# Decode's set-up and first page loads placed in the last heads of prompt attention, sums of probabilities inverted through 32x32 turns, in a hybrid attention and MLP step

## The chip, the cores and the metric

One core of one Trainium2 chip. The metric is the device time of the whole program in microseconds. In these texts PE is TensorE (PEld its weight loads), DVE VectorE, ACT ScalarE, POOL GpSimd, and SP SyncE, whose queue issues the DMAs.

## The reference

One layer of an inference step over a prompt of 16 + 1024 tokens and over 8 sequences with 4 new tokens each, whose past lies in pages:

```python
q, lat, kpe, gb, u = _mixer_inputs(hp, w_in, ...)          # prompt
k, v = _expand_kv(lat, kpe, w_ukv, k_norm_g)
attn = _prompt_attention(q, k, v)                          # 8 heads, causal softmax
xp = _merge_and_ffn(xp, attn, conv, ...)                   # w_o, then a squared-ReLU MLP
# sampled tokens, for each of 8 sequences: 32 pages of 128 past tokens, and 4 new ones
lat_all = concatenate([cache_lat[pages].reshape(past, KV_LORA), lat])
kp_all = concatenate([cache_kpe[pages].reshape(past, QK_ROPE), kp])
k, v = _expand_kv(lat_all, kp_all, w_ukv, k_norm_g)        # keys are RMS-normalised per head
s = where(mask, einsum('qhd,khd->hqk', qs, k) * ATTN_SCALE, -inf)
attn = einsum('hqk,khd->qhd', softmax(s), v)
```

## The kernel before

The program runs five phases in turn, each a block of one instruction stream for every engine, with a barrier of all engines behind each: `inputs`, `prompt_attention`, `sample_attention`, `output_and_mlp`, `store_outputs`. Prompt and sampled tokens share all of them but the two attentions. Within an engine's stream the order is written out by hand, and semaphores couple the engines.

**Prompt attention** goes over heads n = 0 to 7 and, in each, over six steps ("go" 0 to 5). While a head's values are multiplied, the next head's scores are made and the keys and queries of the one after it are turned and split into a rounded and a rest part. In a step PE makes two score blocks of head n+1 (L1325), turns a unit of head n+2 (L1305), and adds two blocks of values of head n (L1361); ACT copies scores out of the accumulators (L1146), exponentiates (L1151) and copies outputs and sums of probabilities (`keep_output`, L1158, L1159); DVE subtracts maxima (L1258) and keeps running ones (L1245, L1247). The sums stand in `g.sums`, 1040 columns on 128 partitions, where all 64 rows of a head hold the same numbers. Heads come in pairs, and in heads 2, 4 and 6 DVE also inverts the sums of the pair before, half a chunk in each of the six steps (`invert_sums`, L1269); POOL then multiplies the outputs (L1103). In head 6 there is no unit to turn, in head 7 no scores are made either. The last pair's inversion stands in the next phase.

**Sample attention** starts with set-up. SP loads the page table and the weight `w_ukv`, then pages, a latent and a rope part each. PE turns 16 pieces of the weight (L1828), ACT copies them (L1554), PE forms the queries in latent space (L1835), DVE and ACT copy and split them (L1645, L1562, L1650) and the weight (`comb_hi` L1557, `comb_lo` L1654), and ACT spreads the rope part (L1564). Then the 32 new tokens' own block: their key norms (L1838, L1560, L1567), scores, mask, maximum, exponential, and first context (L1843 to L1705). DVE's stream also holds the last pair's inversion (L1642) and its multiplication (L1697). All of this stands ahead of the first page. After it come 32 groups of 8 pages: for each page PE turns it (L1896) and expands it to keys and scores (L1906, 12 matmuls), ACT squares (L1614), DVE reduces (L1796). A group's softmax and its context are run one group later. Page buffers are four sets of 8.

## Time and profile before

| | us |
|---|---|
| median of 3 runs (lowest, highest) | 2009.86 (2008.13, 2009.87) |
| profiled execution | 2010.35 |
| its span in the profile | 2008.6 |
| PE busy in the span | 1914.7 |
| DVE, ACT, POOL busy | 962.9, 738.1, 453.9 |

The span runs from the first to the last recorded instruction; the execution's own time is 1.75 us more. The busy times overlap. A duration with "x4" behind it is that of four instructions run one after the other, and a bracket at the end of a row gives the idle time of the engine ahead of it and what ended it.

### The profile page before, as it was taken

The page shows a single profiled execution, that of the slowest core. Times are in us where ns is not written, and L with a number is a line of the kernel's source. Part 1 is how long each engine was busy: PE and PEld are TensorE (multiplying, and loading weights), DVE is VectorE, ACT ScalarE, POOL GpSimd, SP SyncE. Part 2 cuts the span into 40 slices and gives each one's busy share as a digit, 9 for nine tenths or more (in the row PEclk, how much of TensorE's full clock was granted, in tenths as well). Part 3 has the DMA queues.
Part 4 walks back from the last instruction along what each step waited for, and adds up shares of the span by engine and source line. Part 5 has one row for each costly group of instructions (what it writes and reads, how often), then busy time and mean ns, then how long its engine had stood idle before and what let it go on. Part 6 is the DMA issues. An engine that isn't in the chain of part 4 may idle for free. (4 is left out here: it accounts for less than half of the span.)

```text
span 2008.6 us, 36206 instructions
## 1 busy us (share of the span) xinstructions
PE 1914.7 (95%) x12672; PEld 1808.8 (90%) x12672; DVE 962.9 (48%) x1710; ACT 738.1 (37%) x1532; POOL 453.9 (23%) x433
## 2 busy tenths in 40 slices
PE   6999997999779999999998699999999999999998
PEld 5999996777569999999997499999999999999998
DVE  6115034788657777777777733323222322223132
ACT  5111223666446666666666332111111111111011
POOL 3242233232200000000100444222222222122221
PEclk8999998999879999999999599999999999999999
DMA  6122000000122222222222111020211112020202
GB/s 223 43 66 74 11 12 17 1 0 1 39 77 66 74 73 71 71 73 73 73 73 101 42 43 53 18 68 27 58 40 44 52 31 64 24 78 10 73 16 102
DMA packets 180603, 108.47 MB, mean 54 GB/s; under 512 B 52132, under 2 KB 177154, under 8 KB 180276
## 3 DMA queue, kind: packets, MB, share of 16 engines
q1 hardware_dynamic: 180358, 107.21, 18.6%
q8 instruction: 46, 0.75, 0.2%
q10 hardware_dynamic: 174, 0.30, 0.1%
q14 instruction: 25, 0.20, 0.0%
HBM read 97.47 MB, written 10.00 MB: 54 GB/s over the span
## 5 line engine op out<-in xcount | busy, mean ns | idle before, releaser
L1906 PE MATMUL banks<-comb_hi,pageT_hi 128*128 128x272 f32 x1024 | 233.8, 310 | 0.0
L1796 DVE TENSOR_REDUCE k_sums<-k_sq 128x8 f32<-128x512 f32 x256 | 174.3, 681 | 91.3 <-ACT k_sq L1614 91.3
L1906 PE MATMUL banks<-comb_hi,pageT_lo 128*128 128x272 f32 x1024 | 212.3, 289 | 0.0
L1906 PE MATMUL banks<-comb_lo,pageT_hi 128*128 128x272 f32 x1024 | 211.8, 288 | 0.0
L2264 DVE TENSOR_TENSOR xT<-xT,banks 128x1056 f32<-128x1056 f32 x64 | 80.3, 1255 | 272.7 <-PE banks L247 272.7
L1614 ACT ACTIVATE k_sq<-banks 128x512 f32<-128x512 f32 x256 | 152.1, 594 | 141.3 <-PE banks L1906 138.4
L2146 ACT ACTIVATE a_hi<-relu 128x1056 fp32r<-128x1056 f32 x32 | 34.9, 1089 | 388.5 <-DVE relu L2252 388.5
L236 POOL TENSOR_TENSOR w_down_lo<-w_down_raw,w_down_hi 128x512 fp32r<-128x512 f32 x64 | 94.6, 1478 | 339.7 <-ACT w_down_hi L232 339.7
L247 PE MATMUL banks<-hf_hi,w_out_up_hi 128*128 128x352 f32 x768 | 167.1, 326 | 0.0
L247 PE MATMUL banks<-a_lo,w_down_hi 128*128 128x352 f32 x768 | 166.8, 325 | 0.0
L2252 DVE SCALAR_TENSOR_TENSOR relu<-banks,ffn_norm_inv 128x1056 f32<-128x1056 f32 x32 | 40.2, 1258 | 263.8 <-PE banks L247 258.3
L247 PE MATMUL banks<-hf_hi,w_out_up_lo 128*128 128x352 f32 x768 | 166.0, 324 | 0.0
L247 PE MATMUL banks<-a_hi,w_down_lo 128*128 128x352 f32 x768 | 165.8, 324 | 0.0
L247 PE MATMUL banks<-hf_lo,w_out_up_hi 128*128 128x352 f32 x768 | 165.8, 324 | 0.0
L247 PE MATMUL banks<-a_hi,w_down_hi 128*128 128x352 f32 x768 | 165.6, 324 | 0.0
L236 POOL TENSOR_TENSOR w_out_up_lo<-w_out_up_raw,w_out_up_hi 128x1024 fp32r<-128x1024 f32 x40 | 101.5, 2544 | 266.9 <-ACT w_out_up_hi L232 266.9
L1906 PEld LDWEIGHTS banks<-comb_lo,pageT_hi 128*128 128x128 f32 x1024 | 161.3, 189 | 0.0
L1906 PEld LDWEIGHTS banks<-comb_hi,pageT_lo 128*128 128x128 f32 x1024 | 160.7, 189 | 0.0
L1906 PEld LDWEIGHTS banks<-comb_hi,pageT_hi 128*128 128x128 f32 x1024 | 157.7, 190 | 0.0
L247 PEld LDWEIGHTS banks<-hf_hi,w_out_up_hi 128*128 128x128 f32 x768 | 131.4, 190 | 1.1 <-issue 1.1
L247 PEld LDWEIGHTS banks<-hf_hi,w_out_up_lo 128*128 128x128 f32 x768 | 132.3, 188 | 0.0
L247 PEld LDWEIGHTS banks<-a_hi,w_down_hi 128*128 128x128 f32 x768 | 131.4, 188 | 0.0
(382 smaller groups left out, 3813.6 us busy)
## 6 DMA issues: line engine op xcount, KB each, us to landing
page_latents<-in_cache_kv_latent SPq DMA_DIRECT2D x256, 128.0 KB, 2.1
w_out_up_raw<-in_w_up SPq DMA_DIRECT2D x32, 512.0 KB, 4.1
w_down_raw<-in_w_down SPq DMA_DIRECT2D x64, 256.0 KB, 2.7
w_in_raw<-in_w_in SPq DMA_DIRECT2D x17, 512.0 KB, 3.9
x_spill<-xT SPq DMA_DIRECT2D x1, 4296.0 KB, 15.2
xT<-x_spill SPq DMA_DIRECT2D x1, 4296.0 KB, 13.8
page_ropes<-in_cache_k_rope SPq DMA_DIRECT2D x256, 16.0 KB, 1.8
w_out_up_raw<-in_w_o SPq DMA_DIRECT2D x8, 512.0 KB, 4.1
```

Source lines behind the costliest of these rows:

```text
L236: nc.gpsimd.tensor_sub(self.lo[s][:, :, :], self.raw[s][:, :, :], self.hi[s][:, :, :].bitcast(F32)).then_inc(self.lo_done[s], 1)
L247: mm = pe.matmul(out[:, b, 0:self.tb], w[s][:, k, :], x(k)[:, b * self.tb:(b + 1) * self.tb], start=k == 0 and a == 0, stop=k == self.K - ...
L1614: act.activation(sq[j % 2][:, :].rearrange("p (a c) -> p a c", a=2), kn[:, :, 0:WK], ACT.Square)\
L1796: nc.vector.tensor_reduce(ksum[par][:, j, :], sq[j % 2][:, :].rearrange("p (h c) -> p h c", h=H), AX_X, ALU.add)\
L1906: mm = pe.matmul(banks[:, 2 * (j % 2) + half, 0:WC], x[j % AHEAD][:, k, :], w[par][:, k, half, :], start=k == 0 and a == 0, stop=k == KL - ...
L2146: act.activation(a_hi[:, f, :], relu[:, f % 2, :], ACT.Square).then_inc(hi_done, 1)
L2252: nc.vector.scalar_tensor_tensor(blocked(relu[:, s, :]), slot(s)[:, :, 0:OB], 0.0, inv, ALU.max, ALU.mult)\
L2264: nc.vector.tensor_add(x, x, slot(s)[:, :, 0:OB]).then_inc(down.evacuated[s], 1)
```

## The change

The set-up is taken out of `sample_attention`. `prompt_attention` gets an SP stream, which loads `w_ukv` and the page table once head 7's units are turned, and the first two groups of pages once POOL has prepared head 7's values. PE turns the weight in steps 2 to 5 of head 6 (`turn_w`) and forms the latent queries in steps 0 to 3 of head 7; ACT and DVE copy and split beside it, `comb_hi`, `ropes_of_queries`, `strip_fold` and `comb_lo` in head 7. Behind head 7 stand the split of the latent queries and the inversion of the last pair's first chunk (columns 640 to 1039).

`invert_sums` turns a chunk's sums in 32x32 blocks, inverts one column of each block, and turns the inverses back with the one column read 32 times; three DVE instructions a chunk take the place of two reciprocals.

In `sample_attention` the new tokens' block is spread over the page steps of group 0 and the start of group 1 (`new_block`, `new_context`), all in accumulator bank 7. The remaining 640 columns of the last pair are inverted by five reciprocals between the reductions of group 0, and POOL multiplies all 1040 columns in group 1. POOL's constants follow its first copies. The buffers of the moved tensors lie where the token-major queries, keys and values lay.

```diff
+def load_page(g, sp, n, j, q, latents, ropes):
+    lat_cache, rope_cache = g.A["cache_kv_latent"], g.A["cache_k_rope"]
+    page = sp.value_load(g.pages[0:1, ds(n, 1)], min_val=0, max_val=lat_cache.shape[0] - 1)
+    sp.dma_start(latents[:, j, 0:KVL], lat_cache[ds(page, 1), :, :].rearrange("o p n -> p (o n)")).then_inc(g.pages_loaded[q], 16)
+    sp.dma_start(ropes[:, j * ROPE:(j + 1) * ROPE], rope_cache[ds(page, 1), :, :].rearrange("o p n -> p (o n)"))\
+        .then_inc(g.ropes_loaded[q], 16)
...
+    g.sums = low.take("probability_sums", [P, TP + SW - TP % SW], F32)
+    turned_sums = ar.take("turned_sums", [P, (TP - 640) // SW + 1, SW], F32)
+    sum_inv = ar.take("sum_inverses", [P, (TP - 640) // SW + 1], F32)
...
+        @block.sync
+        def _(sp):
+            sp.wait_ge(s["unit_transposed"], H * NU)
+            sp.dma_start(g.wkv[:, :, :], A["w_ukv"].rearrange("(k p) n -> p k n", p=P)).then_inc(s["w_loaded"], 16)
+            sp.dma_start(g.pages[:, :], A["page_table"]).then_inc(s["table_loaded"], 16)
+            sp.wait_ge(s["table_loaded"], 16)
+            sp.wait_ge(s["v_head_ready"], H)
+            for q in range(2):
+                for j in range(PAGE_GROUP):
+                    load_page(g, sp, q * PAGE_GROUP + j, j, q, g.early_pages[q], g.early_ropes[q])
+            sp.wait_ge(s["w_loaded"], 16)
...
+            def keep_w(x):
+                act.wait_ge(s["wT_done"], x + 1)
+                act.copy(g.wukT[0:NOPE, 4 * x:4 * x + 4, :].rearrange("p a c -> p (a c)"), banks[0:NOPE, UNIT_BANK, :])\
+                    .then_inc(s["wT_copied"], 1)
+            def comb_hi(p):
+                act.wait_ge(s["w_loaded"], 16)
+                act.copy(g.comb_hi[p][:, :, :, 0:WK].rearrange("p k a (h c) -> p (k a) h c", c=NOPE),
+                         nope[:, :, 0:NOPE].rearrange("p (a h) c -> p a h c", h=H // 2)).then_inc(s["comb_w_hi"], 1)
+            def ropes_of_queries():
+                act.wait_ge(s["unit_lo_done"], H * NU)
+                for quad in range(4):
+                    act.copy(g.qr4[quad * ROPE:(quad + 1) * ROPE, :, :].rearrange("p b (h s) -> p b h s", h=H),
+                             g.qs[NOPE:QK, :, :].rearrange("p h (b s) -> p b h s", s=SDEC)).then_inc(s["qr_copied"], 1)
...
+                    if is_head(n, H - 2) and go >= 2:
+                        keep_w(go - 2)
+                    if is_head(n, H - 1) and go < 2:
+                        comb_hi(go)
+                    if is_head(n, H - 1) and go == 2:
+                        ropes_of_queries()
...
+                if is_head(n, H - 1):
                     keep_output(n, par, pair, 2)
+                    act.wait_ge(s["qab_copied"], KL)
+                    act.copy(g.qab_hi[:, :, :, :], g.qab[:, :, :, :]).then_inc(s["qab_split"], 1)
...
             def invert_sums(pair, go):
-                c, half = go // 2, go % 2
+                c, back = go // 2, go % 2
                 q0, q1 = CHUNKS[c]
-                mid = (q0 + q1) // 2
-                if half == 0:
+                n = -(-(q1 - q0) // SW)
+                sums = g.sums[:, q0:q0 + n * SW]
+                turn = turned_sums[:, 0:n, :]
+                if not back:
                     v.wait_ge(s["out_copied"], (pair * 2 + 1) * NC + (c + 1))
-                cols = slice(mid, q1) if half else slice(q0, mid)
-                nc.vector.reciprocal(g.sums[:, cols], g.sums[:, cols]).then_inc(s["sums_inverted"], 1)
+                    nc.vector.transpose(turn.rearrange("p a b -> p (a b)"), sums).then_inc(s["sums_turned"], 1)
+                else:
+                    v.wait_ge(s["sums_turned"], pair * NC + (c + 1))
+                    nc.vector.reciprocal(sum_inv[:, 0:n], turn[:, :, 0:1].rearrange("p a o -> p (a o)")).then_inc(s["sums_found"], 1)
+                    v.wait_ge(s["sums_found"], pair * NC + (c + 1))
+                    nc.vector.transpose(sums.rearrange("p (a b) -> p a b", b=SW), sum_inv[:, 0:n].unsqueeze(2).broadcast_to([P, n, SW]))\
+                        .then_inc(s["sums_inverted"], 1)
+            def comb_lo(p):
...
+            def latents_of_queries():
+                v.wait_ge(s["qab_done"], 1)
+                for k in range(KL):
+                    nc.vector.tensor_copy(g.qab[:, :, k, :].rearrange("p b (h s) -> p b h s", h=H),
+                                          banks[:, UNIT_BANK, k * H * NS:(k + 1) * H * NS]
+                                          .rearrange("p (h b s) -> p b h s", b=NSEQ, s=SDEC)).then_inc(s["qab_copied"], 1)
+                v.wait_ge(s["qab_copied"], KL)
+                v.wait_ge(s["qab_split"], 1)
+                nc.vector.tensor_sub(g.qab_lo[:, :, :, :].rearrange("p b k q -> p (b k q)"),
+                                     g.qab[:, :, :, :].rearrange("p b k q -> p (b k q)"),
+                                     g.qab_hi[:, :, :, :].bitcast(F32).rearrange("p b k q -> p (b k q)")).then_inc(s["qab_lo_done"], 1)
             def loop(n, par, pair, norm):
                 if isinstance(n, int) and n == -1:
...
+                    if is_head(n, H - 1) and go == 1:
+                        strip_fold()
+                    if is_head(n, H - 1) and go in (2, 3):
+                        comb_lo(go - 2)
+                if is_head(n, H - 1):
+                    latents_of_queries()
+                    invert_sums(pair, 0)
+                    invert_sums(pair, 1)
...
+            def turn_w(x):
+                if x == 0:
+                    pe.wait_ge(s["w_loaded"], 16)
+                    pe.wait_ge(s["unit_lo_done"], H * NU)
+                else:
+                    pe.wait_ge(s["wT_copied"], x)
+                for i in range(4):
+                    h, k = (4 * x + i) // KL, (4 * x + i) % KL
+                    mm = pe.transpose(banks[0:NOPE, UNIT_BANK, i * P:(i + 1) * P], g.wkv[:, k, h * KW:h * KW + NOPE], ident[:, :])
+                mm.then_inc(s["wT_done"], 1)
+            def latents_of_queries(x):
+                if x == 0:
+                    pe.wait_ge(s["wT_copied"], 4)
+                for h in (2 * x, 2 * x + 1):
+                    for k in range(KL):
+                        at = k * H * NS + h * NS
+                        mm = pe.matmul(banks[:, UNIT_BANK, at:at + NS], g.wukT[0:NOPE, h * KL + k, :], g.qs[0:NOPE, h, :],
+                                       start=True, stop=True)
+                if x == 3:
+                    mm.then_inc(s["qab_done"], 1)
...
+            for q in range(2, SETS):
+                for j in range(G):
+                    load_page(g, sp, q * G + j, j, q, X[q], R[q])
+            with sp.Fori(1, GROUPS // SETS) as i:
                 for q in range(SETS):
+                    sp.wait_ge(s["pages_free"][q], i + 1)
                     for j in range(G):
-                        page = sp.value_load(pages[0:1, ds(i * (SETS * G) + (q * G + j), 1)], min_val=0,
-                                             max_val=n_pool - 1)
-                        if j == 0:
...
+                if is_second(n):
+                    x = g.attnT[:, AW // P - 1, 0:TP]
+                    pool.wait_ge(s["prompt_sums_inverted"], SUM_PIECES)
+                    nc.gpsimd.tensor_mul(x, x, g.sums[:, 0:TP]).then_inc(s["prompt_normed"], 1)
...
+            def new_block(j):
+                s0 = f8(st, NS)
+                s04 = st[0:NS, :, :].rearrange("p b (h s) -> p b h s", h=H)
+                s0T = banks[0:HS, 7, 0:NSEQ * NS].rearrange("p (b t) -> p b t", b=NSEQ)
+                if j == 0:
+                    rope = g.new_page[:, KVL:KVL + ROPE]
+                    nc.vector.tensor_mul(diag[:, :], rope, rope).then_inc(s["k0_parts"], 1)
+                    v.wait_ge(s["k0_parts"], 1)
+                    nc.vector.reduce_sum(rsum[0:NS, 0:1], diag[:, :], AX_X).then_inc(s["k0_parts"], 1)
+                    v.wait_ge(s["sq0_done"], 1)
+                    nc.vector.tensor_reduce(ksum[1][0:NS, 0, :], sq0.rearrange("p (h c) -> p h c", h=H), AX_X, ALU.add)\
+                        .then_inc(s["k0_parts"], 1)
+                    v.wait_ge(s["k0_parts"], 3)
+                    nc.vector.tensor_scalar(rk[0:NS, 0:H], ksum[1][0:NS, 0, :], rsum[0:NS, 0:1], 1.0 / QK, ALU.add, ALU.mult)\
+                        .then_inc(s["k0_parts"], 1)
+                    v.wait_ge(s["k0_parts"], 4)
+                    nc.vector.tensor_scalar(rk[0:NS, 0:H], rk[0:NS, 0:H], EPS, None, ALU.add).then_inc(s["k0_mean"], 1)
+                if j == 2:
+                    v.wait_ge(s["k0_root"], 1)
+                    nc.vector.reciprocal(rk[0:NS, 0:H], rk[0:NS, 0:H]).then_inc(s["k0_inv"], 1)
+                    v.wait_ge(s["s0_done"], 1)
+                    nc.vector.tensor_copy(s0, banks[0:NS, 7, 0:NSEQ * HS]).then_inc(s["s0_steps"], 1)
+                    v.wait_ge(s["s0_steps"], 1)
...
+            def new_context_kept():
+                v.wait_ge(s["l0_done"], 1)
+                v.wait_ge(s["ctx0_copied"], 8)
+            def invert_sums(x):
+                cols = slice(x * P, (x + 1) * P)
+                nc.vector.reciprocal(g.sums[:, cols], g.sums[:, cols]).then_inc(s["prompt_sums_inverted"], 1)
             def soft_mean(n, par):
...
+                    if is_first(n):
+                        new_block(j)
+                        if j in (0, 1, 3, 5, 7):
+                            invert_sums((j + 1) // 2)
+                    if is_second(n) and j == 7:
+                        new_context_kept()
...
+            def new_block(j):
+                if j == 0:
+                    for k in range(KL):
+                        mm = pe.matmul(banks[0:NS, 7, :], g.new_latT[:, k, :], nope[:, k * H:(k + 1) * H, 0:NOPE],
+                                       start=k == 0, stop=k == KL - 1)
+                    mm.then_inc(s["kn0_done"], 1)
+                if j == 1:
+                    pe.wait_ge(s["sq0_done"], 1)
+                    for k in range(KL):
+                        pe.matmul(banks[0:NS, 7, 0:NSEQ * HS], g.new_latT[:, k, :], qab[:, :, k, :], start=k == 0, stop=k == KL - 1)
+                    pe.matmul(banks[0:NS, 7, NSEQ * HS:2 * NSEQ * HS], g.kpe_s[NOPE:QK, :],
+                              g.qs[NOPE:QK, :, :].rearrange("p h (b s) -> p b h s", s=SDEC), start=True, stop=True)\
+                        .then_inc(s["s0_done"], 1)
+                if j == 4:
+                    pe.wait_ge(s["s0_steps"], 4)
+                    for b in range(NSEQ):
+                        mm = pe.transpose(banks[0:HS, 7, b * NS:(b + 1) * NS], st[0:NS, b, :], ident[0:NS, 0:NS])
+                    mm.then_inc(s["s0_transposed"], 1)
+                if j == 6:
+                    pe.wait_ge(s["s0_shifted"], 1)
+                    pe.matmul(banks[:, 7, 2 * NSEQ * NS - NSEQ:2 * NSEQ * NS], fold[0:HS, :, :].rearrange("p a q -> p (a q)"),
+                              mrun[0:HS, :], start=True, stop=True).then_inc(s["m0_spread"], 1)
+                if j == 7:
+                    pe.wait_ge(s["m0_done"], 1)
+                    pe.wait_ge(s["p0_done"], 1)
+                    for b in range(NSEQ):
+                        mm = pe.transpose(banks[0:NS, 7, b * HS:(b + 1) * HS], sc[1][0:HS, b, :], ident[0:HS, 0:HS])
+                    mm.then_inc(s["p0_transposed"], 1)
+            def new_context():
+                pe.wait_ge(s["p0_copied"], 1)
+                pe.wait_ge(s["m0_done"], 1)
+                for a in range(2):
+                    mm = pe.matmul(banks[:, 7, a * KVL:(a + 1) * KVL], pr[0:NS, 4 * a:4 * a + 4, :].rearrange("p b q -> p (b q)"),
+                                   g.new_page[:, 0:KVL], start=True, stop=True)
+                mm.then_inc(s["ctx0_done"], 1)
             def spread_max(n):
...
+                    if is_second(n) and j == 0:
+                        new_context()
                     if soft is not None:
                         if j == 5:
+                            if is_second(n):
+                                pe.wait_ge(s["ctx0_copied"], 8)
                             transpose_max(soft[0])
                         if j == 6:
```

## Rows read from the trace of the kernel before

**Rows 1.** The page: the span, and busy time of each engine with its share.

```profile
span 2008.6 us, 36206 instructions
...
PE 1914.7 (95%) x12672; PEld 1808.8 (90%) x12672; DVE 962.9 (48%) x1710; ACT 738.1 (37%) x1532; POOL 453.9 (23%) x433
```

**Rows 2.** Busy time by stretch: PE, PEld, DVE, ACT, POOL; TensorE's clock; DMA.

```profile
490.00:530.00 40.00, 36.48 (x185) 26.47 (x184) 32.42 (x75) 24.72 (x46) 8.73 (x12) 0.96 0.00 1
...
545.00:556.31 11.31, 9.36 (x44) 8.52 (x42) 1.45 (x1) 3.75 (x3) 0.00 (x0) 0.50 0.34 90
556.31:575.10 18.79, 8.91 (x33) 3.78 (x32) 11.25 (x24) 7.71 (x15) 2.18 (x7) 0.59 0.31 80
...
575.10:591.30 16.20, 15.54 (x109) 15.17 (x110) 7.32 (x15) 7.41 (x23) 0.00 (x0) 0.84 0.33 85
564.00:575.10 11.10, 3.83 (x22) 2.54 (x22) 7.66 (x20) 3.79 (x9) 2.18 (x7) 0.50 0.31 81
...
607.00:623.00 16.00, 16.00 (x138) 15.11 (x137) 12.55 (x32) 10.93 (x31) 1.44 (x4) 1.00 0.28 74
```

**Rows 3.** Timeline from the last prompt copy to the first page: start, duration, engine, line, [idle].

```profile
537.36 0.37 ACT L1159 COPY attnT<-banks 64x256 f32<-64x256 f32 x1
538.54 0.25 SPq L1469 DMA_DIRECT2D page_table<-in_page_table  x1
...
539.80 6.64 DVE L1642 RECIPROCAL probability_sums<-probability_sums 128x1040 f32<-128x1040 f32 x1
...
543.78 3.62 PE L1828 MATMUL banks<-ident,w_ukv 128*64 128x128 f32 x16 [7.15 <-DMA w_ukv<-in_w_ukv]
...
549.35 7.03 PE L1835 MATMUL banks<-q_sampled,w_ukT 64*128 64x32 f32 x32 [1.95 <-ACT w_ukT L1554]
...
568.07 0.60 PE L1848 MATMUL banks<-ident,scaled_scores 32*32 32x32 f32 x8 [6.69 <-DVE scaled_scores L1685]
...
575.16 1.09 PE L1896 MATMUL banks<-ident,page_latents 128*128 128x128 f32 x4 [1.98 <-ACT context L1575]
```

**Rows 4.** Instructions grouped by line, 320 to 538 us.

```profile
L1269 DVE RECIPROCAL probability_sums<-probability_sums 128x200 f32<-128x200 f32 (+2 forms) x18 | 22.0, 1222 | 0.0
```

**Rows 5.** Timeline, ACT: the one exponential of 832 columns of heads 0, 1 and 5.

```profile
366.31 0.88 ACT L1151 ACTIVATE scoresT<-scoresT 128x832 f32<-128x832 f32 x1
...
388.70 0.88 ACT L1151 ACTIVATE scoresT<-scoresT 128x832 f32<-128x832 f32 x1
...
484.06 0.88 ACT L1151 ACTIVATE scoresT<-scoresT 128x832 f32<-128x832 f32 x1
```

**Rows 6.** Timeline inside the last head.

```profile
524.63 1.91 PE L1361 MATMUL banks<-scoresT,v_and_ones 128*128 128x400 f32 x4 [2.23 <-ACT attnT L1159]
...
533.15 0.48 ACT L1158 COPY probability_sums<-banks 64x400 f32<-64x400 f32 x1 [2.44 <-PE banks L1361]
```

**Rows 7.** Timeline, 549 to 562 us: set-up instructions that the change moves.

```profile
549.20 1.99 ACT L1557 CAST comb_hi<-w_ukv 128x1024 fp32r<-128x1024 f32 x2
...
560.47 0.60 ACT L1562 CAST q_latent_hi<-q_latent 128x512 fp32r<-128x512 f32 x1
...
561.09 1.68 ACT L1564 COPY q_rope<-q_sampled 32x256 f32<-32x256 f32 x4
561.17 0.69 DVE L1650 TENSOR_TENSOR q_latent_lo<-q_latent,q_latent_hi 128x512 fp32r<-128x512 f32 x1 [4.00 <-ACT q_latent_hi L1562]
561.78 2.35 DVE L1654 TENSOR_TENSOR comb_lo<-w_ukv,comb_hi 128x1024 fp32r<-128x1024 f32 x2
```

**Rows 8.** Timeline, SyncE's queue: two page loads in a row.

```profile
541.00 0.39 SPq L1479 DMA_DIRECT2D page_latents<-in_cache_kv_latent  x1
...
542.78 0.34 SPq L1479 DMA_DIRECT2D page_latents<-in_cache_kv_latent  x1
```

**Rows 9.** Timeline, DVE: the last pair's scaling, and half of the first contexts.

```profile
569.95 1.23 DVE L1697 TENSOR_TENSOR attnT<-attnT,probability_sums 128x1040 f32<-128x1040 f32 x1
...
573.29 1.77 DVE L1705 COPY context<-banks 32x256 f32<-32x256 f32 x4 [1.79 <-PE banks L1860]
```

323 lines of the change are left out of this document (132 added, 191 removed).

## The prediction

> **What bounds the kernel now.** I read the page first: PE is busy for 1914.7 of 2008.6 us [rows 1], so some 94 us of the whole program are not covered by matmuls, and a change can win by filling such holes or by shortening what sets PE's pace. Busy time by stretch then shows two kinds of stretch. In the page groups (607 to 623 us) PE is busy all of 16.00 us at the full clock, with DVE at 12.55, ACT at 10.93 and POOL at 1.44 [rows 2]: PE sets the pace there, and each matmul added costs its time. In prompt attention (490 to 530 us) PE has 36.48 of 40 us and DVE 32.42 [rows 2], two engines that wait for each other in turns. The third place is the seam between the attentions. The timeline there has the last prompt copy ending at 537.73 us and the first page's transposes starting at 575.16 [rows 3]. These 37.43 us are a chain: the weight's load (PE idle for 7.15), its transposes, a copy, 32 small matmuls, then the new tokens' block, in which PE waits for DVE for 6.69 us [rows 3]. The clock granted is 0.50 of full, the 1.2 GHz level, while the set-up matmuls run (545.00 to 556.31), so even PE's busy 9.36 us there are slow ones [rows 2]. The expensive thing is the order of small steps on an otherwise empty chip, and the change takes this order apart.
>
> **The seam itself.** After the change nothing of that chain stands ahead of the first page, and its page has been loaded. What remains are the steps behind ACT's last copy: the split of the latent queries, 0.60 us on ACT and 0.69 on DVE [rows 7], then DVE's turn, inversion and turn of one chunk. A turn of 416 columns is not in this trace. Its nearest rows: the multiplication of 1040 columns between SBUF tiles at 1.23 us, or 1.18 ns a column [rows 9], and the reciprocal of 1040 columns at 6.64 us, or 6.4 ns a column [rows 3]. I take the first, since a turn only moves data and the reciprocal is the one DVE operation here that works on a column many times over: 0.49 us a turn. The inversion of 13 columns is 0.2. With five handovers between the steps at some 0.06 us each that makes 0.60 + 0.69 + 2 x 0.49 + 0.2 + 0.3 = 2.8 us. The barrier costs what it did, 537.73 to 538.54 = 0.8 [rows 3], and the first instruction 0.1 more. So 37.4 us become 3.7: a gain of 33.7. A lower bound of the turn is nothing (2.7 left), the upper the reciprocal's rate (2 x 2.66 instead of 2 x 0.49, 8.0 left).
>
> The Trainium skill (Vector Engine (DVE) Microarchitecture Reference, the section on the reshape front-end) says that the transposing array is pipelined to sustain one element per cycle per lane, which sides with the low price. By its figure the estimate for 416 columns would be some 0.43 us and the sum 0.1 us lower; no row here shows it.
>
> Do the loads hold the seam instead? SP issues a page (latent and rope) every 1.78 us [rows 8], so 16 pages need 28.5 us. They start when POOL has prepared head 7's values, in step 2 of head 6, at about 512 us in this trace (head 5's exponential of 832 columns is at 484.06 [rows 5], a head is 22 to 24 us long, and that step is some 4 us on). The last is issued at about 540, against DVE's end at 540.5, and with head 7 longer the distance grows. SP's queue is just not the last one.
>
> **Inversions inside prompt attention.** 18 reciprocals of 1222 ns on average [rows 4], 7.3 us of DVE for each pair. After: twice 1056 columns of turns at 1.18 ns, 2.5 us, and three inversions of 8 to 13 columns, 0.5, together 3.0. What is DVE time worth? The marker of 832 columns comes once a head. Heads 0 to 1, with no inversion between, lie 388.70 - 366.31 = 22.39 us apart. From head 1 to head 5 are 484.06 - 388.70 = 95.36 us for four heads, 5.80 over four times 22.39, with two inversions in them [rows 5]: 2.9 us a pair for 7.3 us of DVE. So more than half of it is hidden now. If the cost goes in proportion, 3.0 us of DVE cost 1.2 and 1.7 are won; if the slack of 4.4 us swallows them, all 2.9. I take 2.2, twice: 4.4 us. The third pair's inversion lies in head 6; there the units' splits are missing already and DVE is less pressed: 1.0 (bounds 0 and 2.9). If turns went at the reciprocal's rate, a pair would need 13.7 us instead of 7.3.
>
> **What heads 6 and 7 take on.** Head 6: 16 transposes, 3.62 us at half clock [rows 3], 1.8 at full, with four ACT copies. They go where other heads have the transposes and splits of a unit, PE work of the same kind, so I cost them at nothing; without that cover it is the 1.8 us of PE. One effect stays: the last copy of the weight now stands ahead of the output copy for which head 7's first values wait (2.23 us already [rows 6]), another 0.6 (a copy of 64 rows and 400 columns takes ACT 0.48 [rows 6], this one has 512). Head 7: the 32 matmuls are 7.03 us at half clock [rows 3], four batches of 1.76, or 0.9 at full. The first batch fits the idle 2.23 us. The other three stand ahead of values on PE, which in the last head leads: ACT waits 2.44 us for it at 533.15 [rows 6]. They cost 3 x 0.9 to 3 x 1.76, 2.6 to 5.3. ACT's casts (1.99) and rope copies (1.68) and DVE's subtractions (2.35) [rows 7] and strip fold (0.6) go into waits of these engines such as the 2.44; uncovered they would be 3.7 and 3.0. The head grows by 3.2 to 5.9 us; I take 4.2, the small matmuls at somewhat above the full clock's price. Prompt attention together: -4.4 - 1.0 + 4.2 = -1.2 us.
>
> **What groups 0 and 1 take on.** The new tokens' block is 8.91 us of PE between 556.31 and 575.10, at a mean clock of 0.59 with nearly all of its matmuls at half [rows 2]. At full clock that is 4.5, and since PE is the pace in page groups, it is all paid. DVE: 7.66 us from 564.00 to 575.10 [rows 2], less the 1.23 of the scaling that goes to POOL and the 1.77 of context copies that go to ACT [rows 9], so 4.7; and five reciprocals of 128 columns at 6.4 ns and 0.1, 4.6. Group 0 uses 7.32 us of DVE now in 16.20 [rows 2] (it has no softmax of a group before it), so 16.6 of the new 16.2 + 3.5 = 19.7. DVE doesn't bind over the group, but its extra work comes in lumps, and PE's stream now has waits in it: for the scaled scores in step 4, the shifted ones in step 6, the maxima in step 7. Everything of the next pages is queued behind these. I walked the chain: DVE reaches the end of step 3 about 1 us after PE wants it, and is in time for the rest. With handovers 1.7 us. ACT gets 4 us and two table loads, into 7.41 of 16.20; POOL's scaling of 1040 columns has a group to itself. Group 0 and 1 together: +6.2 (bounds 4.5, nothing lost to waits, and 11, when DVE's 9.3 are paid in full with 1.7 beside them). PE starts the pages after a pause, as now, and the slow first page of group 0 stays.
>
> A rule speaks against POOL's part. The Trainium skill (SBUF — State Buffer, the section "Who interferes with whom") has a DVE operation with two SBUF inputs and a POOL operation lock each other out of a shared port pair. By it, DVE's short operations on the scores would wait for up to one scaling, some 2.6 us once. The trace shows no such pair at one time in the groups; DVE's 12.55 of 16.00 would take it in, so the sum stays.
>
> **The sum.** -33.7 - 1.2 + 6.2 = -28.7 us. The profiled execution of 2010.35 lies 0.5 over the median; its 2010.35 - 28.7 = 1981.7 gives 1981.2 against the median of 2009.86, -1.4%. A measurement of this kernel tells some 0.2%, 4 us, from no change.
>
> **Rivals.**
> 1. *The holes take the set-up whole.* Head 7's added work disappears in waits (+1.0 for 4.2), the groups pay only matmuls (4.5). For it: both attentions have idle ACT and DVE time. Against: PE itself leads in head 7. 28.7 + 3.2 + 1.7 = 33.6 won, 1976.3.
> 2. *The lumps become waits.* Head 7 grows by 8, because ACT's and DVE's 3.7 and 3.0 us stand ahead of exponentials and subtractions on the chain, and groups 0 and 1 by 11. For it: in head 7 nearly every step waits for another engine. 28.7 - 3.8 - 4.8 = 20.1, 1989.8.
> 3. *SP's queue holds the seam.* The block can't end before the 16th page is issued. If a page took 2.5 us instead of 1.78, the last would be out at 552, 11 us late: 1992. Against: 1.78 is measured with the same instructions.
> 4. *Slower: turns cost more than reciprocals.* At 6.4 ns a column three pairs cost 3 x 6.4 more than before instead of winning 5.4, and the seam 4.3 more, together 28.9: 2010, no change. Beyond 6.4 ns a column it decides for slower; at 8 ns about 2021. Nothing in the rows says that a pure move is that slow.
>
> **How the numbers follow.** My forecast (1977 to 1987) has 0.60, rival 1 0.16, rival 2 0.18, rival 3 0.03, rival 4 0.03. The range of 8 in 10 reaches from 1974 to 1990, over rival 1's 1976.3 and rival 2's 1989.8. Faster by over 0.2%: 0.96; within 0.2%: 0.02; slower: 0.02.
>
> **What would show it.** In the changed profile: some 4 us instead of 37.4 from the last prompt copy to the first page's transposes; DVE turns of 0.5 us; head markers 45 to 46 us apart over two heads instead of 47.7; head 7 longer by about 4 us; group 0 near 20 us. The prediction is wrong if the turns are several times dearer, if PE waits for DVE in each of group 0's steps, or if the seam is held by a queue I call just in time.

## The result and the profile after

The changed kernel takes 1984.93 us in the median of 4 runs (1983.62 to 1985.58), against 2009.14 us (2008.13 to 2009.87, 4 runs): a ratio of 0.9878, with a 95% interval of 0.9866 to 0.9889. It is 24.2 us faster where 28.7 were forecast, and 3.7 us above the predicted 1981.2. The profiled execution took 1985.29 us, with a span of 1983.6, so the two spans are 25.0 us apart; the forecast was made of spans, and so is what follows.

The page of the changed kernel, the lines that answer to [rows 1]:

```profile
span 1983.6 us, 36199 instructions
...
PE 1904.1 (96%) x12672; PEld 1801.8 (91%) x12672; DVE 949.6 (48%) x1722; ACT 738.8 (37%) x1539; POOL 455.9 (23%) x434
```

The timeline of the changed kernel from the last prompt copy to the first page, which answers to [rows 3]:

```profile
540.03 0.37 ACT L1210 COPY attnT<-banks 64x256 f32<-64x256 f32 x1
540.42 0.62 ACT L1259 CAST q_latent_hi<-q_latent 128x512 fp32r<-128x512 f32 x1
541.14 0.69 DVE L1377 TENSOR_TENSOR q_latent_lo<-q_latent,q_latent_hi 128x512 fp32r<-128x512 f32 x1 [4.71 <-ACT q_latent_hi L1259]
541.75 0.60 DVE L1347 STREAM_TRANSPOSE turned_sums<-probability_sums 128x416 f32<-128x416 f32 x1
542.39 0.24 DVE L1350 RECIPROCAL sum_inverses<-turned_sums 128x13 f32<-128x13 f32 x1
542.66 0.61 DVE L1352 STREAM_TRANSPOSE probability_sums<-sum_inverses 128x416 f32<-128x416 f32 x1
544.22 0.24 POOL L1666 CAST comb_hi<-q_latent_hi 128x64 fp32r<-128x64 f32 x1 [15.27 <-POOLq L327]
...
545.18 1.09 PE L2020 MATMUL banks<-ident,page_latents 128*128 128x128 f32 x4 [5.87 <-PEq L327]
```

The seam is what the change says: 37.43 us have become 540.40 to 545.18 = 4.78. Two pieces are left in it. From the last copy to DVE's last turn at 543.27 are 2.87 us, one chain of five short instructions; from there to PE's first matmul are 1.91, the barrier and the start of the streams. PE's line names the barrier itself (PEq) and no transfer.

ACT's exponential of 832 columns comes once a head. Its lines in heads 1 and 5 of the changed kernel, which answer to [rows 5]:

```profile
389.18 0.89 ACT L1202 ACTIVATE scoresT<-scoresT 128x832 f32<-128x832 f32 x1
...
480.74 0.88 ACT L1202 ACTIVATE scoresT<-scoresT 128x832 f32<-128x832 f32 x1
```

With such marks the whole span can be laid out. "First context" and "last context" are PE's first and last matmuls of `page_latents` with `probabilities` (L1880 before, L2004 after), at 608.11 and 1101.57 us before and at 585.80 and 1079.75 after. Each row is the difference of two marks:

| stretch | before, us | after, us | difference | forecast |
|---|---|---|---|---|
| start to head 1's exponential | 388.70 | 389.18 | +0.5 | 0 |
| head 1 to head 5 | 95.36 | 91.56 | -3.8 | -4.4 |
| head 5 to the last copy's end | 53.67 | 59.66 | +6.0 | +3.2 |
| the seam | 37.43 | 4.78 | -32.7 | -33.7 |
| first page to first context | 32.95 | 40.62 | +7.7 | +6.2 |
| first to last context (L1880, L2004) | 493.46 | 493.95 | +0.5 | 0 |
| the rest of the program | 907.03 | 903.85 | -3.2 | 0 |
| sum | | | -25.0 | -28.7 |

The forecast missed by 3.7. The two largest misses are head 5 to the last copy (2.8 too low) and the rest of the program (3.2 the other way, so it hides as much). The experiments go after the first of them; the second is looked at behind them.

### The profile page after: what moved, and what is told of

It reads as the page before. It is cut to its first block and busy times, and to the rows that moved or that the text cites. A ratio compares the mean times of both kernels' runs of the same rounds, so it can differ in the third digit from the quotient of the medians.

```text
span 1983.6 us, 36199 instructions
## 1 busy us (share of the span) xinstructions
PE 1904.1 (96%) x12672; PEld 1801.8 (91%) x12672; DVE 949.6 (48%) x1722; ACT 738.8 (37%) x1539; POOL 455.9 (23%) x434
```

## The experiments

Each ratio is to the kernel before, which was measured beside it on the same chip (medians of 2009.14 to 2010.17 us, so a difference of two medians of this table carries about 1 us of that). The start of the program up to head 1's exponential, which no experiment touches, took 386.1 to 389.2 us in the profiled executions. Spans therefore compare to about 3 us, and the readings below go by differences of marks inside one trace.

| kernel | median us | ratio | 95% interval | span us |
|---|---|---|---|---|
| the change | 1984.93 | 0.9878 | 0.9866 to 0.9889 | 1983.6 |
| turned_only | 2000.52 | 0.9962 | 0.9948 to 0.9976 | 2001.5 |
| plain_inverses | 1988.43 | 0.9899 | 0.9883 to 0.9916 | 1985.3 |
| late_loads | 1997.73 | 0.9936 | 0.9920 to 0.9953 | 1997.6 |
| front_block | 1992.53 | 0.9917 | 0.9901 to 0.9934 | 1985.7 |
| latents_twice, two runs | 1989.02 | 0.9897 | 0.9877 to 0.9916 | 1986.4 |
| filled | 1980.32 | 0.9851 | 0.9835 to 0.9868 | 1980.0 |
| casts_early | 1979.44, one run | | | 1977.7 |
| tail | 1981.78 | 0.9858 | 0.9841 to 0.9874 | 1980.3 |
| tail_early | 1979.50 | 0.9854 | 0.9838 to 0.9871 | 1977.7 |
| early_filled | 1976.26 | 0.9830 | 0.9817 to 0.9844 | 1974.5 |
| seam_filled | 1976.12 | 0.9836 | 0.9823 to 0.9850 | 1973.5 |

### The turned inversions alone

The kernel before, with nothing but the turns in the inversions of heads 2, 4 and 6; the last pair is still inverted whole at the seam.

```diff
-                cols = slice(mid, q1) if half else slice(q0, mid)
-                nc.vector.reciprocal(g.sums[:, cols], g.sums[:, cols]).then_inc(s["sums_inverted"], 1)
+                if not back:
+                    nc.vector.transpose(turn.rearrange("p a b -> p (a b)"), sums).then_inc(s["sums_turned"], 1)
+                else:
+                    nc.vector.reciprocal(sum_inv[:, 0:n], turn[:, :, 0:1].rearrange("p a o -> p (a o)"))...
+                    nc.vector.transpose(sums.rearrange("p (a b) -> p a b", b=SW), sum_inv[:, 0:n].unsqueeze(2).broadcast_to([P, n, SW]))...
```

> The kernel before with one thing changed: the sums of the three pairs in heads 2, 4 and 6 are turned, inverted once and turned back; everything else, the last pair's reciprocal too, is as before. Theory 1 (the inversion pays by itself what the two traces show between the head markers): heads 1 to 5 take 91.6 us instead of 95.4, head 6 about 1 us less, in all -4.5 to -5.5 us, some 2004 us against 2009. Rival (part of the 3.8 us comes from elsewhere in the changed program, such as the moved tiles): less than 2.5 us.

It took 2000.52 us, 8.7 less than the 2009.23 of the kernel before beside it. By its marks head 1 to head 5 is 480.13 - 388.60 = 91.53 us (-3.8), head 5 to the last copy's end 531.17 - 480.13 = 51.04 (-2.6). That is -6.5 in prompt attention (the profiled execution, 2003.18 us, is the slowest of the five); its seam of 568.54 - 531.17 = 37.37 us is the old one. What DVE's relief took away can be read in PE's waits. First the waits of the kernel before, 366 to 537 us, then those of this one (PE's wait, its cause, total, times, longest):

```profile
PE banks L1361 <- ACT attnT L1159: 5.4, 7, 2.2
PE banks L1341 <- POOL max_diagonal L1095: 1.7, 3, 0.7
PE banks L1305 <- DVE q_lo L1202: 1.4, 4, 0.5
PE banks L1325 <- DVE running_max L1247: 0.7, 3, 0.3
```

```profile
PE banks L1373 <- ACT attnT L1162: 6.1, 7, 2.5
PE banks L1317 <- DVE q_lo L1207: 1.4, 4, 0.5
```

The waits for `max_diagonal` and `running_max`, both at the end of DVE's chain, are gone, 2.4 us of them, while the one for ACT's copies grew by 0.7. That is only a part of what was won: over heads 1 to 5 PE's idle time fell from 5.47 to 3.78 us, and its busy time, with 501 matmuls recorded in both, from 89.89 to 87.75. The rows don't say why the busy part fell. Of the 2.6 us behind head 5 some are something else. Busy time and TensorE's clock from 525 to 530 us, first in the kernel before, then here (PE, PEld, DVE, ACT, POOL, granted clock, DMA share, GB/s):

```profile
525.00:530.00 5.00, 5.00 (x13) 2.77 (x12) 2.75 (x8) 2.81 (x5) 0.61 (x1) 0.66 0.01 3
```

```profile
525.00:530.00 5.00, 5.00 (x22) 3.42 (x21) 0.62 (x2) 2.36 (x5) 0.00 (x0) 1.00 0.00 0
```

The kernel before spends 2 x (1 - 0.66) x 5 = 3.4 us of its last head at the 1.2 GHz level, and this one none (the 5 us ahead of these have 1.00 in both). PE is busy throughout that stretch, so 3.4 us at half the rate do 1.7 us of work: 1.7 of the 2.6 are the clock, and about 1.0 is the third pair's inversion. This is the first sign that the clock matters in the last head. It also explains in part why my expectation for this kernel, made without the clock, was low. It need not be the turns' doing: PE waits in this kernel's last head too, for 2.46 us where the kernel before waits for 2.23 [rows 6], and yet its clock stays at 1.00 from 500 us to the last copy:

```profile
519.77 1.58 PE L1373 MATMUL banks<-scoresT,v_and_ones 128*128 128x400 f32 x4 [2.46 <-ACT attnT L1162]
```

### The inversions put back

The change, with each half chunk inverted by a plain reciprocal as before.

```diff
-                    nc.vector.transpose(turn.rearrange("p a b -> p (a b)"), sums).then_inc(s["sums_turned"], 1)
-                    ...
+                cols = slice(mid, q1) if back else slice(q0, mid)
+                nc.vector.reciprocal(g.sums[:, cols], g.sums[:, cols]).then_inc(s["sums_inverted"], 1)
```

> The changed kernel with the two plain reciprocals a chunk back, in heads 2, 4 and 6 and behind head 7. Theory 1: heads 1 to 5 again 95.4 us (+3.8), head 6 +1 to +2, the seam +1.3 (two reciprocals of 200 columns, 2.8 us, for 1.5 us of turns), together +6 to +7, some 1991 us. Rival (in head 6 and at the seam other engines hide it): +4, the heads 1 to 5 alone.

1988.43 us, 3.5 more than the change. Heads 1 to 5 are 481.53 - 386.12 = 95.41 us, again those of the kernel before, so 3.85 are lost there. The seam grows by 1.1, to 545.75 - 539.84 = 5.91. In this timeline the two reciprocals of 200 columns stand where the changed kernel has a turn, an inversion and a turn:

```profile
541.19 2.66 DVE L1346 RECIPROCAL probability_sums<-probability_sums 128x200 f32<-128x200 f32 x2
```

2.66 us against 1.52 (541.75 to 543.27). From head 5 to the last copy it has 539.84 - 481.53 = 58.31 us, less than the changed kernel's 59.66, of which 1.7 are the clock: it spends 3.4 us of head 7 at the lower level, where the changed one spends 6.9. Without the clock's part it is 0.4 longer there. So once the set-up lies in heads 6 and 7, the third pair's turned inversion is worth 0.4 and not 1.0 us. Together the three are 5.4, less 1.7 of the clock 3.7, beside the median's 3.5; I had expected 6 to 7.

### The page loads put back

SP's first two sets of pages are issued in the sample attention's block, as before; all else as changed.

```diff
-            sp.wait_ge(s["v_head_ready"], H)
-            for q in range(2):
-                for j in range(PAGE_GROUP):
-                    load_page(g, sp, q * PAGE_GROUP + j, j, q, g.early_pages[q], g.early_ropes[q])
...
-            for q in range(2, SETS):
+            for q in range(SETS):
```

> The changed kernel with the loads of the first two page groups issued at the start of the page phase, and only the weight and the page table loaded in head 6. Theory 1 (the early loads are needed once the set-up is gone from the seam): PE's first transposes wait until eight pages are issued at 1.61 us each and landed, 15 us into the phase instead of 1.9, +13 us, some 1998. Rival (a page is enough, or the pages come faster than PE takes them): +2 to +4.

The median is 12.8 us above that of the change. Its last copy ends at 540.78 and the first page's transposes are these:

```profile
559.06 1.12 PE L2016 MATMUL banks<-ident,page_latents 128*128 128x128 f32 x4 [19.38 <-DMA page_latents<-in_cache_kv_latent]
```

The seam is 18.28 us, 13.5 more than 4.78, and PE waits for the first latent page by name. So of the 32.7 us won at the seam, the moved set-up alone brings 19.2 and the early loads the other 13.5. In head 5 to the last copy it differs from the change only by the clock (61.23 us with 10.2 at the lower level, 59.66 with 6.9). The loads beside prompt attention cost PE nothing there.

### The new tokens' block put in front

All eight steps of the new tokens' block ahead of group 0's first page instead of one behind each page.

```diff
                 if is_first(n):
+                    for j in range(G):
+                        new_block(j)
...
-                    if is_first(n):
-                        new_block(j)
```

> The changed kernel with the new tokens' block run in one piece ahead of group 0's pages (its context still in group 1). Theory 1 (spread over group 0 it costs PE its matmuls and about 1.3 us of waits, 7.7 us with the context; in one piece it is a chain of three engines at the slow clock, some 13 us before the contexts): seam +13, groups -5, +7 to +9 us, some 1993. Rival (the lumps in group 0 cost as much as the chain did): within 2 us.

The median is 7.6 us above the change's. In PE's timeline of this kernel the block is alone again:

```profile
540.55 3.58 PE L1959 MATMUL banks<-w_ukv,new_latT 128*32 128x512 f32 x4 [5.85 <-PEq L327]
544.80 1.05 PE L1965 MATMUL banks<-q_latent,new_latT 128*32 128x256 f32 x4 [0.68 <-ACT w_ukT L1691]
...
548.24 0.60 PE L1972 MATMUL banks<-ident,scaled_scores 32*32 32x32 f32 x8 [1.84 <-DVE scaled_scores L1809]
...
551.18 1.12 PE L2023 MATMUL banks<-ident,page_latents 128*128 128x128 f32 x4
```

The first page starts 10.6 us later after the last copy (535.80 to 551.18 = 15.38 against 4.78), and the stretch from it to the last context is 4.8 shorter (529.80 against 534.57): spreading the block over the pages is worth 5.8 us by the marks. The profiled execution is the fastest of this kernel's four (1987.43, the others 1992.47 to 1994.44), and unlike the change's its clock stayed at full in head 7 (56.41 us from head 5 to the last copy, against 59.66), so the two spans are only 2.1 apart. The same matmuls in the changed kernel, among the pages:

```profile
550.10 1.96 PE L1956 MATMUL banks<-w_ukv,new_latT 128*32 128x512 f32 x4
553.86 1.05 PE L1962 MATMUL banks<-q_latent,new_latT 128*32 128x256 f32 x4
...
561.28 0.40 PE L1969 MATMUL banks<-ident,scaled_scores 32*32 32x32 f32 x8 [0.27 <-DVE scaled_scores L1808]
...
570.06 1.12 PE L1986 MATMUL banks<-new_page,probabilities 32*128 32x256 f32 x4
...
581.18 0.30 PE L1997 MATMUL banks<-ident,maxima 128*128 128x128 f32 x1 [0.73 <-issue]
```

The first is nearly halved where it stands among the pages (3.58 to 1.96), by when the clock has come back, and the small ones with it (0.60 to 0.40). The second took the same in either place, 1.05. With the groups left out (0.61, 0.38 and 0.40) the seven add up to 5.92 us, and the waits in this part of the stream to 0.27 + 0.73 = 1.00.

### The latent queries' matmuls twice

The 32 small matmuls of head 7 are each made twice, with the same result.

```diff
+                        for _ in range(2):
-                        mm = pe.matmul(banks[:, UNIT_BANK, at:at + NS], ...
+                            mm = pe.matmul(banks[:, UNIT_BANK, at:at + NS], ...
```

> The changed kernel with each of the 32 small matmuls of the latent queries issued twice in head 7. Theory 1 (PE's own work is what lengthens head 7): three batches in full and part of the first, +3.2 to +5 us. Rival (ACT's casts and DVE's subtractions ahead of exponentials are): under 1.5 us.

4.1 us more than the change in the median; head 5 to the last copy is 543.43 - 480.44 = 62.99 us, 3.3 more, at the same share of the lower clock (6.8 us of it against 6.9). A doubled batch takes 1.97 us at the full clock and a single one 1.07 (below), so each of the four adds 0.90, together 3.6: PE pays for nearly all of every batch. PE leads in head 7, as the prediction had it.

### The clock in the last head held up

The changed kernel's PE in the last head, in order (only matmuls, some left out), and the two stretches of 5 us:

```profile
521.05 1.07 PE L1500 MATMUL banks<-q_sampled,w_ukT 64*128 64x32 f32 x8 [1.50 <-ACT w_ukT L1215]
522.13 2.22 PE L1479 MATMUL banks<-scoresT,v_and_ones 128*128 128x400 f32 x4
...
524.70 1.91 PE L1500 MATMUL banks<-q_sampled,w_ukT 64*128 64x32 f32 x8
```

```profile
520.00:525.00 5.00, 3.95 (x16) 2.48 (x16) 2.35 (x8) 4.93 (x9) 0.83 (x1) 0.79 0.35 90
525.00:530.00 5.00, 5.00 (x14) 3.33 (x13) 3.02 (x7) 2.35 (x4) 0.61 (x1) 0.52 0.34 92
```

PE waits for the last copy of the turned weight for 1.50 us; a few us later the same eight matmuls take 1.91 instead of 1.07, and the clock is at the lower level for 2 x 0.21 x 5 + 2 x 0.48 x 5 = 6.9 us. The experiment gives PE two matmuls whose results nobody reads, in the place where it would wait:

```diff
+                    if is_head(n, H - 1) and go == 0:
+                        ...
+                        for w in (512, 256):
+                            pe.matmul(banks[:, 0, 0:w], g.ones[:, :], g.wkv[:, 0, 0:w], start=True, stop=True)
```

> The changed kernel with two matmuls more on PE in step 0 of head 7, of 512 and 256 columns, ahead of the wait for the weight's copy; their results are not read. Theory 1 (PE's wait there is followed by 6.9 us at the 1.2 GHz level, which lengthens the head by about half of that; with the wait filled the clock stays): the latent queries' second batch takes 1.07 us instead of 1.91, the granted clock between head 7's start and end is 1.00, and the head is 2.5 to 3.5 us shorter, some 1982. Rival (the slow stretch does not hang on that wait): no stretch gets faster, time unchanged or up to 1.5 us longer.

It is 4.6 us faster than the change in the median, by doing more, and its slowest execution (1981.70) is below the change's fastest (1983.62). In its timeline the added matmuls take most of the wait, and the second batch of small matmuls keeps its price; the clock is whole in both stretches:

```profile
519.19 1.46 PE L1527 MATMUL banks<-w_ukv,ones 128*128 128x512 f32 x4
520.85 1.07 PE L1500 MATMUL banks<-q_sampled,w_ukT 64*128 64x32 f32 x8 [0.21 <-ACT w_ukT L1215]
...
523.65 1.07 PE L1500 MATMUL banks<-q_sampled,w_ukT 64*128 64x32 f32 x8
```

```profile
520.00:525.00 5.00, 4.79 (x26) 3.37 (x25) 3.16 (x10) 4.93 (x10) 0.83 (x1) 1.00 0.32 77
525.00:530.00 5.00, 5.00 (x23) 2.92 (x21) 4.63 (x8) 4.30 (x8) 0.61 (x1) 1.00 0.37 97
```

Head 5 to the last copy is 536.94 - 480.52 = 56.42 us, 3.2 less than the changed kernel's 59.66. The clock's own share is half of 6.9, 3.4, so the rows agree.

One profile could be chance, since the clock differs between executions. Over all profiles it goes like this. The four with the wait filled (this one, casts_early, early_filled, seam_filled) have no lower level in the last head. Of the seven with the set-up moved and the wait left open, six have it: 3.4 us (plain_inverses, whose wait is 1.73 us, and tail_early, 0.60 us), 6.8 or 6.9 (the change, latents_twice, tail) and 10.2 (late_loads); front_block, with the same 1.50 us, has none. So filling the wait holds the clock, but an open wait is not always followed by a fall, and its length does not tell how long the lower level lasts.

### The weight's casts moved to head 6

Filled, with ACT's two casts of the weight (1.99 us) in head 6 instead of head 7.

```diff
-                    if is_head(n, H - 1) and go < 2:
+                    if is_head(n, H - 2) and go < 2:
                         comb_hi(go)
```

> The kernel with the filled wait in step 0 of head 7, and ACT's two casts of the weight (1.03 us each) moved from steps 0 and 1 of head 7 to steps 0 and 1 of head 6. Theory 1 (PE leads in head 7, the casts lie in ACT's waits): from head 6's marker to the last output copy 34.6 us as without the move, within 0.5. Rival (ACT's work stands ahead of exponentials on the path): 1 to 2 us shorter.

In one run, 1979.44 us. Head 5 to the last copy is 534.41 - 478.01 = 56.40 us against filled's 56.42. From head 6's exponential of 832 columns to the last copy are 33.94 us instead of 34.57, a little outside the 0.5 that I had allowed, but head 5's to head 6's grew as much, from 21.85 to 22.46. That is the mark itself, which stands behind the casts on ACT. PE did not feel it: from head 5's exponential to its first small batch in head 7 are 40.31 us (40.33 in filled), from there to the last copy's end 16.09 in both. So the casts cost PE nothing in either head.

### The tail shortened

The split of the latent queries on ACT is put ahead of the last output copies (step 4 of head 7), and DVE does the chunk's turns first and its subtraction last. No value changes.

```diff
+                    if is_head(n, H - 1) and go == 4:
+                        act.wait_ge(s["qab_copied"], KL)
+                        act.copy(g.qab_hi[:, :, :, :], g.qab[:, :, :, :]).then_inc(s["qab_split"], 1)
...
                     keep_output(n, par, pair, 2)
-                    act.wait_ge(s["qab_copied"], KL)
-                    act.copy(g.qab_hi[:, :, :, :], g.qab[:, :, :, :]).then_inc(s["qab_split"], 1)
```

> The changed kernel with the end of head 7 in another order: ACT splits the latent queries in step 4, ahead of its last output copies, and DVE inverts the last chunk before it takes the split's rest. Theory 1 (the 2.9 us of DVE behind the last output copy are bare): DVE ends by 540.6 us instead of 543.3, -2.5 us, some 1982.4. Rival (the next block's start on TensorE, 1.9 us behind DVE's end where the other engines need 0.9, waits for something else than DVE): under 1 us.

3.15 us below the change in the median. Its timeline at the seam:

```profile
537.84 0.68 DVE L1380 TENSOR_TENSOR q_latent_lo<-q_latent,q_latent_hi 128x512 fp32r<-128x512 f32 x1
...
539.58 0.37 ACT L1210 COPY attnT<-banks 64x256 f32<-64x256 f32 x1
540.87 0.24 POOL L1670 CAST comb_hi<-q_latent_hi 128x64 fp32r<-128x64 f32 x1 [12.42 <-POOLq L327]
...
541.83 0.63 PE L2024 MATMUL banks<-ident,page_latents 128*128 128x128 f32 x4 [2.98 <-PEq L327]
```

The last copy now ends last of all, at 539.95, and PE starts 1.88 us later. The chain of 2.9 us behind it is gone entirely, and the 1.9 of barrier and start stand alone: POOL's first instruction comes 0.92 us after the copy, PE's another 0.96 later.

### The weight turned a step earlier

The tail's kernel, with the four turns of the weight and their copies one step earlier in head 6, and the latent queries in three steps of head 7, not four.

```diff
-                    if is_head(n, H - 2) and go >= 2:
-                        turn_w(go - 2)
-                    if is_head(n, H - 1) and go < 4:
-                        latents_of_queries(go)
+                    if is_head(n, H - 2) and 1 <= go < 5:
+                        turn_w(go - 1)
+                    if is_head(n, H - 1) and go < 3:
+                        for x in ((0, 1), (2,), (3,))[go]:
+                            latents_of_queries(x)
```

> As the reordered end, and the weight is turned in steps 1 to 4 of head 6 instead of 2 to 5, the first two batches of latent queries stand in step 0 of head 7 and the others in steps 1 and 2. Theory 1 (PE's small batches in head 7 are paid one by one, but step 0 has a wait of 1.5 to 2.2 us): the batch that ran at the slow clock (1.91 us) is hidden and the copy of the weight no longer delays the first values (0.6): -2 to -3 us beside the reordered end alone, some 1980. Rival (PE's total work in heads 6 and 7 is what counts, wherever it stands): within 1 us of the reordered end.

2.3 us below the tail in the median. Head 5 to the last copy is 536.90 - 480.38 = 56.52 us, 3.15 less, of which the clock is 1.7 (3.4 us at the lower level, not 6.9) and 1.4 the removed wait. The groups gave 1.0 back: 580.05 - 538.75 = 41.30 us from the first page to the first context, not 582.14 - 541.83 = 40.31. That is the clock again. The first 8 us of the pages, in the tail's kernel and in this one:

```profile
541.83:549.83 8.00, 7.29 (x34) 5.33 (x35) 2.86 (x8) 2.53 (x7) 4.44 (x10) 0.79 0.33 92
```

```profile
538.75:546.75 8.00, 7.50 (x26) 4.76 (x27) 2.22 (x6) 2.20 (x6) 4.48 (x10) 0.60 0.29 76
```

The first has 3.4 us at the lower level and the second 6.4, and the first page's transposes take 0.63 and 1.09 us. PE's wait ahead of them is the same, 2.98 and 2.95 us. What makes the clock fall sooner after it in one than in the other, no run tells.

### Both together, and the seam filled too

First the last kernel with one matmul of 256 columns at the start of head 7; then this with one more of 512 columns after head 7's last values, so that PE works until the barrier.

```diff
+                    if is_head(n, H - 1) and go == 0:
+                        ...
+                        for w in (256,):
+                            pe.matmul(banks[:, 0, 0:w], g.ones[:, :], g.wkv[:, 0, 0:w], start=True, stop=True)
```

> The reordered end, the weight turned one step earlier with two batches in step 0 of head 7, and one matmul of 256 columns more in that step's wait. Theory 1 (the 3.4 us that ran at the 1.2 GHz level in head 7 go back to full): -1.5 us against the same kernel without the extra matmul, some 1978. Rival (two batches already hold the clock in other executions, and the fill only delays the values): 0 to +0.5.

```diff
+                    if is_head(n, H - 1) and go == GOES - 1:
+                        pe.matmul(banks[:, 0, 0:512], g.ones[:, :], g.wkv[:, 0, 0:512], start=True, stop=True)
```

> As the one before, with one matmul of 512 columns more behind head 7's last values, while ACT still copies. Theory 1 (the clock falls in PE's wait at the seam, and group 0's first pages run at half until 550; one more matmul shortens the wait from 3.1 to 2.1 us): up to -2 us if the clock stays, and the first page is expanded in 1.8 us instead of 3. Rival (2 us are long enough for it to fall): no change.

The first is 1976.26 us (1973.89 to 1976.36), 3.2 below the kernel without the filler and 8.7 below the change. The last head keeps its full clock, and head 5 to the last copy is 534.39 - 479.43 = 54.96 us, 1.56 less; another 1.1 are the groups, 40.21 instead of 41.30, which have 3.4 us at the lower level like the tail's, and those the filler in head 7 is not shown to have brought. The second brings nothing: 1976.12 us, with overlapping ranges. PE's wait at the barrier is 2.10 us instead of 2.96, since PE is kept busy longer, but it ends no sooner after the others. PE's first page in the second kernel:

```profile
535.54 0.63 PE L2032 MATMUL banks<-ident,page_latents 128*128 128x128 f32 x4 [2.10 <-PEq L327]
```

From the last copy's end to the page are 1.86 and 1.85 us, and to the first context another 40.21 and 40.41. The first 8 us of the pages have a clock of 0.79 in both, so the fall came later and lasted as long. The slow part at the start of the groups is not bought off in this way.

## Why the prediction was right, and where it was off

**The seam: right, 1.0 too much.** 32.7 us were won for the forecast 33.7. The chain behind the last copy took 2.87 us where 2.8 stood. Its terms were off in ways that cancel: a turn of 416 columns takes 0.60 us and not 0.49, with the handovers shorter than the 0.06 each that I had put in. The other piece is wrong: I took 0.8 for the barrier and 0.1 for the first instruction, from a row of SP's queue, and PE needs 1.91. The tail's kernel separates it: 1.88 us with nothing else in them. In the kernel before, PE's start was hidden behind its wait for the weight. Worked out from the rate that the Trainium skill (Vector Engine (DVE) Microarchitecture Reference, the section on the reshape front-end) gives for its transposing array, one element per cycle per lane, my estimate for such a turn was 0.43 us. The trace has 0.60, so the measurement decides. A turn still comes nearer to a move than to a reciprocal, and rival 4, which needed a turn at the reciprocal's rate, is out.

**The inversions: right.** -3.8 us over heads 1 to 5 where 4.4 were forecast, shown from both sides (91.53 with the turns alone, 95.41 with them taken out). All ten chunks up to 544 us, grouped by line, cost DVE this:

```profile
L1352 DVE STREAM_TRANSPOSE probability_sums<-sum_inverses 128x416 f32<-128x416 f32 (+2 forms) x10 | 5.5, 552 | 0.3
L1347 DVE STREAM_TRANSPOSE turned_sums<-probability_sums 128x416 f32<-128x416 f32 (+2 forms) x10 | 5.4, 536 | 0.0
L1350 DVE RECIPROCAL sum_inverses<-turned_sums 128x13 f32<-128x13 f32 (+2 forms) x10 | 2.2, 217 | 0.0
```

13.1 us for ten chunks, 1.31 a chunk or 3.9 a pair, where I had 3.0 and the kernel before 7.3. A saving of 3.4 of DVE's time a pair gave 1.9 of the program's, a share of 0.56; I had let 2.2 of 4.3 through, 0.51. The rate was right, the size of the turns was low. For the third pair 1.0 was forecast. Without the clock's part it is 1.0 alone and 0.4 beside the set-up.

**Heads 6 and 7: the step that was off.** Without the clock's part (half of the time at the lower level), head 5 to the last copy is 52.0 us before, 51.0 with the turns alone, 56.6 with the set-up alone and 56.2 after. The set-up in heads 6 and 7 costs 4.6 (52.0 to 56.6) to 5.2 (51.0 to 56.2), and I had 4.2. Its parts stand as far as they were tried: PE pays the small matmuls nearly in full (doubled, they cost 3.3 more), ACT's casts nothing. The 0.4 to 1.0 us beyond my 4.2 have no experiment of their own. What I did not have is the clock. I had priced the set-up's matmuls "at somewhat above the full clock's price", but not what comes after the wait of 1.50 us that the copy of the weight makes PE take: 6.9 us at the lower level against 3.4 before, at half a us each 1.75. Together 6.0 where 3.2 stood. That filling the wait keeps the clock up is shown: none of the four filled profiles has the lower level there, six of the seven others with the moved set-up have it, and filled, the same work is 3.2 us shorter. Whether and how long the clock falls after an open wait is not the kernel's alone: the profiled execution of the kernel with the block in front had no lower level in head 7, though it has the same wait, nor had that of the turns alone behind its 2.46 us, and the late loads' one had 10.2 us of it. So the 1.75 are what two profiled executions differ by, and the change itself may cost less or more than that in others.

**Groups 0 and 1: right in kind, 1.5 short.** 7.7 us where 6.2 were forecast. The block's matmuls are paid in full, but they are 5.9 and not 4.5. I halved 8.91 as if nearly all of it had run at the half clock, from a mean of 0.59 over a stretch in which PE is idle for half of the time [rows 2]. Cut finer, the kernel before had its full clock back for two of the matmul groups. One of them in its timeline, and the stretch of both:

```profile
559.73 1.11 PE L1843 MATMUL banks<-q_latent,new_latT 128*32 128x256 f32 x4
```

```profile
559.70:561.40 1.70, 1.68 (x7) 0.53 (x5) 0.23 (x1) 1.40 (x3) 0.00 (x0) 0.94 0.13 33
```

They took 1.11 and 0.61 there, and 1.05 and 0.61 after the change: nothing could be halved in them.

The other 1.75 are waits and handovers, of which 1.00 have a row; 1.7 were forecast. DVE did not bind: PE's waits for it there are the 0.27 and the 0.5 for the second page, which was there before as well.

**SP's queue and the port: no part.** The first of the 16 early pages is issued at 508.13 (I had about 512) and the last at 533.58, 6.8 us ahead of the last copy's end. Most are 1.61 us apart; with two longer steps the mean is 1.70. My 1.78 was the first step of the kernel before, whose next ones are 1.70 and 1.69.

```profile
508.13 0.38 SPq L982 DMA_DIRECT2D page_latents<-in_cache_kv_latent  x1
...
509.82 0.34 SPq L982 DMA_DIRECT2D page_latents<-in_cache_kv_latent  x1
...
511.43 0.34 SPq L982 DMA_DIRECT2D page_latents<-in_cache_kv_latent  x1
...
533.58 0.34 SPq L982 DMA_DIRECT2D page_latents<-in_cache_kv_latent  x1
```

Rival 3 is out. As for the port pair that DVE and POOL share, POOL's scaling ran from 574.65 to 576.68, and every DVE instruction in that stretch read one SBUF operand at most beside one in the accumulators. The case that I had taken from the Trainium skill (SBUF — State Buffer, "Who interferes with whom"), a DVE operation with two SBUF inputs beside POOL's, did not arise, and no run here shows what it costs.

**What nobody had in the sum.** The rest of the program got 3.2 us shorter though its code is the same. It is the clock, once inside the MLP and once behind it. Two stretches of the kernel before, 80 and 100 us long, have a granted clock of 0.98, and the same stretches of the changed one, 21.8 us earlier, 1.00. The first of them, before and after:

```profile
1221.57:1301.57 80.00, 79.46 (x479) 77.39 (x478) 26.13 (x19) 16.02 (x19) 23.28 (x10) 0.98 0.12 34
```

```profile
1199.75:1279.75 80.00, 79.46 (x489) 77.40 (x488) 27.38 (x20) 16.66 (x20) 23.96 (x11) 1.00 0.11 32
```

0.02 of 180 us is 3.6. Cut finer, the kernel before has two falls, each within 10 us that have a mean of 0.83, and each right behind a wait of PE: 0.54 us for `ffn_norm_inv` (its matmul starts at 1255.30) and 2.41 us at the barrier ahead of the output (1992.37). All 13 profiles have both waits. The first fall is in two of them, the kernel before and the one with the turns alone (2001.5 - 1094.93 = 906.6 us for this part), and in none of the eleven with the set-up moved, which take 903.7 to 905.1 (the filled one 1980.0 - 1076.22 = 903.8). The second is in those two and in five of the eleven. So it is the same as in head 7: a wait is followed by a fall in some profiles and not in others. Where this part begins does not decide it, for the late loads' kernel begins it at 1093.91 and has neither. Whether the first fall belongs to the kernels whose set-up is in the old place or to chance, one profile of each can't tell. Without this part's 3.2 the change would stand at 1984.9 + 3.2 = 1988.1, still inside the range. The miss would then be 6.9 us and not 3.7, and that it isn't is luck.

The forecast's case, then, came true in its mechanism. Heads 6 and 7 grew by 6.4 to 7.0 with the clock's part (4.2 forecast, 8 in rival 2) and the groups by 7.7 (6.2, and 11 in rival 2). In head 7 the size is near rival 2's, but not for its reason: what it held against the chain, ACT's casts among it, costs nothing there as far as it was tried.
